# Context tokens' gated projections and mixing laid as filler products between those of norms, expansion, rotation and attention

## The reference, cut to what matters

```python
# first block: h is 272 tokens
h = h + 0.5 * swiglu(rms_norm(h, g_ffn1), ...)
h = h + hybrid_mixer(rms_norm(h, g_mix), ...)   # in_proj, norms, expansion, rope, 16 heads, out
h = h + 0.5 * swiglu(rms_norm(h, g_ffn2), ...)
# second block, layer 0
mod_l = silu_c @ ada_w[0] + ada_b[0]            # shifts, scales and gates of the 256 tokens
mod_c = silu_cc @ ada_w[0] + ada_b[0]           # the same for the 256 context tokens
hl = rmsnorm(x, norm1_g) * (1 + sc1) + sh1
hc = rmsnorm(ctx, norm1_g) * (1 + csc1) + csh1
yl, yc = gmlp_mixer(hl, *gp), gmlp_mixer(hc, *gp)

def gmlp_mixer(h, w_in, b_in, ln_g, ln_b, w_s, b_s, w_out, b_out):
    z = gelu(h @ w_in + b_in)                   # 1024 -> 4096
    u, v = split(z, 2)
    v = layernorm(v, ln_g, ln_b)
    v = einsum('gpq,bcqgd->bcpgd', w_s, v in chunks of 128 tokens, 16 groups) + b_s
    return (u * v) @ w_out + b_out
```

## Time and profile before

| | |
|---|---|
| median of 3 runs | 3289.74 us (3283.09 to 3289.74) |
| profiled execution | 3290.62 us, span 3288.9 us |
| mean granted TensorE clock over the span | 0.912 |
| TensorE busy | 2795.8 us (85% of the span) |
| VectorE, ScalarE, GpSimd busy | 1086.0, 506.4, 320.2 us |

### The profile page before, as it was taken

One profiled execution on the slowest core, in us unless ns is written; L12 is line 12 of the kernel. 1 busy time (PEld: TensorE's weight loads), 2 busy tenths in 40 slices (PEclk: granted clock), 3 DMA queues, 4 the chain that ended last, 5 costly groups with the idle time before them and its releaser, 6 DMA issues. The chain is left out here.

```text
span 3288.9 us, 58163 instructions
## 1 busy us (share of the span) xinstructions
PE 2795.8 (85%) x25453; PEld 1936.1 (59%) x25453; DVE 1086.0 (33%) x2184; ACT 506.4 (15%) x1106; POOL 320.2 (10%) x356
## 2 busy tenths in 40 slices
PE   8998989899998997787777499798888976977775
PEld 7887735788684544444444234388888964544443
DVE  4562363256414412210000321365655522101002
ACT  1000122100110101000000200154444411000001
POOL 1000000000000000211111100042222201111110
PEclk9999755899999998898999799799999987999998
DMA  8684100378523204999999521000000019999994
GB/s 285 225 249 127 39 26 1 128 255 256 153 77 115 64 26 164 347 396 402 404 405 406 182 64 48 18 4 3 4 4 3 4 53 345 403 407 408 405 405 187
DMA packets 279491, 616.54 MB, mean 187 GB/s; under 512 B 28916, under 2 KB 181703, under 8 KB 245204
## 3 DMA queue, kind: packets, MB, share of 16 engines
q1 hardware_dynamic: 237584, 539.56, 44.5%
q10 hardware_dynamic: 30068, 58.82, 5.0%
q0 software_dynamic: 11600, 14.59, 1.4%
HBM read 612.76 MB, written 21.08 MB: 193 GB/s over the span
## 5 line engine op out<-in xcount | busy, mean ns | idle before, releaser
L2076 PE MATMUL bank<-expert_weights,ex_xt 128*64 128x256 f32 x2688 | 314.2, 389 | 92.7 <-DMA expert_weights<-in_moe_w_up_dram 73.4
L2076 PEld LDWEIGHTS bank<-expert_weights,ex_xt 128*64 128x64 f32 x2688 | 215.5, 140 | 206.0 <-issue 136.5
L527 PE MATMUL bank<-u,weights 128*128 128x272 f32 (+1 forms) x1408 | 317.6, 389 | 10.3 <-DVEq L550 10.3
L527 PEld LDWEIGHTS bank<-u,weights 128*128 128x128 f32 x1408 | 269.9, 192 | 57.7 <-DVEq L550 10.9
L1228 DVE SCALAR_TENSOR_TENSOR ada_acc<-ada_w,cond,ada_acc 128x512 f32 (+1 forms) x336 | 227.5, 744 | 1.6 <-PEq L499 1.6
L1987 DVE TENSOR_TENSOR ex_hidden<-ex_silu,bank 128x256 f32<-128x256 f32 x64 | 26.9, 421 | 595.9 <-ACT ex_silu L2125 595.9
L605 PE MATMUL bank<-rw_mixed,weights 128*128 128x512 f32 (+2 forms) x448 | 189.3, 584 | 31.7 <-DVEq L616 28.2
L2076 PE MATMUL bank<-weights,ex_xt 128*64 128x256 f32 x1408 | 166.0, 392 | 35.0 <-DMA weights<-in_moe_w_up_dram 33.6
L2097 PE MATMUL bank<-expert_weights,ex_hidden_turned 128*64 128x512 f32 x672 | 160.3, 621 | 21.7 <-DVE ex_hidden_turned L1990 21.7
L2076 PEld LDWEIGHTS bank<-weights,ex_xt 128*64 128x64 f32 x1408 | 112.2, 141 | 95.3 <-issue 56.5
L605 PEld LDWEIGHTS bank<-rw_mixed,weights 128*128 128x128 f32 (+1 forms) x448 | 84.2, 189 | 137.2 <-issue 135.3
(11 more groups left out here) (550 smaller groups left out, 4138.2 us busy)
## 6 DMA issues: line engine op xcount, KB each, us to landing
expert_weights<-in_moe_w_gate_dram SPq DMA_DIRECT2D x84, 1024.0 KB, 24.5
expert_weights<-in_moe_w_up_dram SPq DMA_DIRECT2D x84, 1024.0 KB, 24.5
expert_weights<-in_moe_w_down_dram SPq DMA_DIRECT2D x84, 1024.0 KB, 24.7
ada_w<-in_ada_w_dram ACTq DMA_DIRECT2D x24, 2048.0 KB, 9.0
weights<-in_moe_w_gate_dram SPq DMA_DIRECT2D x44, 1024.0 KB, 24.2
weights<-in_moe_w_up_dram SPq DMA_DIRECT2D x44, 1024.0 KB, 24.3
weights<-in_moe_w_down_dram SPq DMA_DIRECT2D x44, 1024.0 KB, 24.4
weights<-in_w_gate_dram SPq DMA_DIRECT2D x22, 1024.0 KB, 5.5
```

The source lines that it names most:

```text
L527: last = nc.tensor.matmul(k.bank[b + side * NB][:, 0:N], w[:, f, c * P:(c + 1) * P], rhs[:, f, 0:N], start=(f == 5), stop=(f == 4))
L2076: last = nc.tensor.matmul(half_cols(k.bank[2 + side], t), xt[:, s, f * SLOTS:(f + 1) * SLOTS], w[:, q * 512 + t * 256:q * 512 + t * 256 + ...
```

## The change

The gated block's work for the context tokens, up to the gated product, moves ahead of the first model's attention output.

- The weights' order gets two segments more: cv (8 tiles of w_in's second half) behind in, and cu (8 tiles of the first half) behind expand. w_in is thus read twice, 16 MB more.
- Layer 0's mods are summed by `row_sums` (24 products of 512 columns) in the mix norm instead of by column sums in the four small norms; they are turned and spread at the start of in_proj. `mark` moves from layer 1 to layer 0.
- in_proj also normalizes the context tokens (`csq`, 8 products with ones after its second chunk) into `hc`.
- Class `Ahead` lays the v projection, 128 products of 256 columns (128 columns of stationary), in pieces: 16 in each of fqn, fkn, cq and ckv, 64 in the expansion; and the u projection, 128 products as well: 48 in the row norms, 32 in the rotation, 48 in attention (2, 2, 1, 2, 1 over the units to unit 29). Results are drained by VectorE, from rotation on by ScalarE.
- Gelu of v runs on ScalarE in the expansion, centering and squares in the row norms, the normalizing passes (two of 512 columns a unit) on VectorE in units 0 to 7 of attention. The spatial weights are turned in units 8 to 11 (4 transposes each) and mixed in from unit 13, two products of 128 columns a unit. Gelu of u and the gate lie in attn_out.
- Attention's scores get two PSUM banks instead of three, its mixed values two instead of three; the expansion's values are made between the heads.
- gm_norm, gm_v, gm_u, its norm and the spatial stage handle 256 tokens instead of 512. gm_out reads the two halves from two tensors, as two products of 256 columns.
- One `k.clear()` more stands behind attn_out.

```diff
@@ norm_stage, tensor
             for c in range(kc):
+                if ahead is not None:
+                    ahead.v_pieces(pe, 2)
                 pe.wait_ge(squared, c + 1)
                 last = nc.tensor.matmul(ps, k.ones[:, :], sq[:, c, w], start=(c == 0), stop=(c == kc - 1))
             last.then_inc(summed, 1)
-            if mods is not None and mods.l == 0:
-                mods.sums(mods.share_of_norm)
-            if mods is not None and mods.l == 1:
+            if mods is not None:
                 mods.row_sums(pe)
+            if ahead is not None:
+                ahead.v_pieces(pe, 2 * DC - 2 * kc)
@@ head_norm_stage, tensor
             for c in range(heads):
+                ahead.v_pieces(pe, 2)
                 pe.wait_ge(squared, c + 1)
...
-            if mods is not None:
-                mods.sums(14)
+            ahead.v_pieces(pe, 2 * DC - 2 * heads)
@@ expand_stage, sync and tensor
+            for _ in range(4):
+                ahead.feed_v(sp)
...
             for h in range(HEADS):
+                ahead.v_pieces(pe, DC)
+                if h < 6:
+                    values(h)
@@ row_norm_stage, tensor
                     nc.tensor.matmul(k.bank[n][0:HEADS, 0:N], of[0:r, c, :], sq[0:r, i % 4, 0:N],
                                      start=(c == 0), stop=(c == chunks - 1)).then_inc(summed, 1)
+                    ahead.u_pieces(pe, 1)
+            ahead.u_pieces(pe, 8)
...
+                    nc.tensor.matmul(k.bank[2 + i % 4][0:r, 0:N], to[:, c, 0:r], stat[:, n, 2, 0:N],
                                      start=True, stop=True).then_inc(sent, 1)
+                    ahead.u_pieces(pe, 1 + i % 2)
@@ rope_stage, tensor
                 nc.tensor.matmul(k.bank[n % 4][0:QK, 0:TA], k.rope_turn[0:QK, 0:QK], x[0:QK, h, :],
                                  start=True, stop=True).then_inc(turned, 1)
+                ahead.u_pieces(pe, 2)
@@ attention_stage, tensor
+                if u < 30:
+                    ahead.u_pieces(pe, (2, 2, 1, 2, 1)[u % 5])
+                if 8 <= u < 12:
+                    ahead.turn(pe, u - 8)
+                if 13 <= u < 13 + GC:
+                    ahead.spread(pe, u - 13)
@@ attention_stage, vector
+                if u < 8:
+                    ahead.v_norm(dve, 2 * u, 2 * u + 2)
+                if 14 <= u < 14 + GC:
+                    ahead.keep_spread(dve, u - 14)
@@ class Ahead
+    def feed_v(self, sp):
+        j = self.v_fed
+        self.v_fed += 1
+        sp.wait_ge(self.v_made, 2 * j + 2)
+        self.k.stream.start_number(sp, self.k.seg["cv"].first + j + RING)
...
+    def v_pieces(self, pe, count):
+        k = self.k
+        for _ in range(count):
+            n, f = divmod(self.v_at, DC)
+            j, t = divmod(n, 2)
+            self.v_at += 1
+            if f == 0:
+                if t == 0:
+                    k.stream.wait(pe, k.seg["cv"], j // RING, j % RING)
+                if n >= 8:
+                    pe.wait_ge(self.v_kept, n - 1)
+                elif n >= 4:
+                    pe.wait_ge(self.v_kept, n - 3)
+            last = k.nc.tensor.matmul(self.v_bank(n), self.hc[:, f, t * P:(t + 1) * P],
+                                      k.stream.slot(k.seg["cv"], j)[:, f * 256:(f + 1) * 256],
+                                      start=(f == 0), stop=(f == DC - 1))
+            if f == DC - 1:
+                last.then_inc(self.v_made, 1)
...
+    def spread(self, pe, g):
+        k = self.k
+        if g == 0:
+            pe.wait_ge(self.wt_copied, 4)
+            pe.wait_ge(self.v_normed, 8)
+        else:
+            pe.wait_ge(self.mix_kept, g)
+        for t in range(2):
+            last = k.nc.tensor.matmul(k.bank[6][:, t * P:(t + 1) * P], self.v[:, t, g * P:(g + 1) * P], self.wt[:, g, :],
+                                      start=True, stop=True)
+        last.then_inc(self.mixed, 1)
@@ gmlp_v_stage
-        units = [(j, t) for j in range(seg.tiles) for t in range(4)]
+        units = [(j, t) for j in range(seg.tiles) for t in range(2)]
```

More of the change, by code:

```diff
@@ L407, in place_params, with norm_stage @@
             at += pieces[0][0].shape[0]
-def norm_stage(k, name, src, kc, width, eps, parts, dst, scratch=None, mods=None, loads=None):
+def norm_stage(k, name, src, kc, width, eps, parts, dst, scratch=None, mods=None, loads=None, ahead=None):
     nc = k.nc
@@ L426, in norm_stage @@
             block.sync(loads)
+        if ahead is not None:
+            block.sync(ahead.feed_v)
         @block.scalar
@@ L470, in _ @@
                                                    op0=ALU.mult, op1=ALU.mult).then_inc(ready, 1)
-            if mods is not None and mods.l == 0 and mods.columns == 6 * DC:
-                mods.spread(dve)
+            if ahead is not None:
+                ahead.keep_v(dve)
             if parts[0][3] is not None:
@@ L613, in linear_stage @@
             block.gpsimd(pool)
+        if scalar is not None:
+            block.scalar(scalar)
         def empty(eng):
@@ L776, in _, with row_norm_stage @@
                                                op0=ALU.mult, op1=ALU.mult)
-def row_norm_stage(k, name, sides, per, width, mods=None):
+            ahead.keep_v(dve)
+def row_norm_stage(k, name, sides, per, width, ahead):
     nc = k.nc
@@ L795, in row_norm_stage, with _ @@
         rows = [side[2] for side in sides]
+        @block.sync
+        def _(sp):
+            ahead.feed_u(sp, 0, 3)
         @block.gpsimd
@@ L988, in _ @@
             nc.scalar.activation(g[:, 1, :], g[:, 1, :], ACT.Ln, bias=1.0).then_inc(adone, 1)
+            for _ in range(4):
+                ahead.keep_u_scalar(act)
         @block.vector
@@ L1037, in keys, with _ @@
             return META + (t + 1) * P
+        @block.sync
+        def _(sp):
+            ahead.feed_u(sp, 5, 6)
+            ahead.load_spatial_bias(sp)
+            ahead.feed_u(sp, 6, 8)
         @block.tensor
@@ L1237, in last_share @@
         self.add(dve, self.begun - 1, self.ROUND - self.ROUND // self.rest, self.ROUND)
-    def sums(self, count):
-        nc = self.k.nc
-        for m in range(self.columns, self.columns + count):
-            for v in range(2):
-                last = nc.tensor.matmul(self.k.bank[7][:, 2 * m + v:2 * m + v + 1],
-                                        self.acc[:, v, m * P:(m + 1) * P], self.k.ones[:, 0:1], start=True, stop=True)
-        self.columns += count
-        last.then_inc(self.summed, 1)
-        self.parts += 1
     def mark(self, dve):
@@ L1289, in spread_rows @@
         self.gains()
-    def spread(self, dve):
-        k, nc, l = self.k, self.k.nc, self.l
-        mod = k.mods[l]
-        link = Chain(dve, self.done)
-        dve.wait_ge(self.summed, self.parts)
-        for v in range(2):
-            link(nc.vector.tensor_tensor(mod[:, v, :], k.bank[7][:, v:12 * DC:2],
-                                         param(k, "ada_b", 6 * DC, 6 * DC * l), ALU.add))
-        self.gains()
     def gains(self):
@@ L1322, in ffn @@
+def ffn(k, n, h, u, T, t0, seg, gains, to, acc):
     nc = k.nc
```

458 lines of the change are left out of this document (348 added, 110 removed).

## The result

The changed kernel takes 3250.15 us (median of 4 runs, 3243.80 to 3264.11), the one before 3288.47 us on the same chip (4 runs, 3283.09 to 3289.74). The ratio is 0.9892, 95% interval 0.9863 to 0.9921: 1.1% faster, 38 us where 55 were forecast. The profiled execution took 3252.20 us (span 3250.5) against 3290.62, so the two traces differ by 38.4 us.

A forecast was written before the change was run, and what follows sets the result against it. TensorE was taken as the bound: dense products at full clock in the gated block, narrow ones at half clock earlier. Terms of -121.6 and +66.2 sum to -55.4, so 3290.6 becomes 3235 us; range 3195 to 3268.

The forecast's parts named there:

- rival 4: Weight tiles come late at the doubled pace or in the shared ring, one landing in each of three stages: 3250; chance 0.05.
- the likeliest 3215 to 3250: Whole kernel: the main case, its span from the bound on the gaps and 10 us on attention; chance 0.64.
- a clock of 0.50 in attention: Attention: a sign that would make the forecast wrong, which expected near 1.00 from the expansion to unit 30.
- the row norms with no gap: Row norms: the lower bound, where changes between product shapes cost nothing, +8.7 us instead of +20.1.
- gaps of 0.41 and 0.33: Expansion: a head's gaps at half and full clock, used to claim that attention's gaps keep some 0.77 at full clock.
- rival 3: TensorE stays at 1.2 GHz through attention as well: attention takes 178 us, +67; chance 0.04.
- 2.4 of stall, 0.5 of start: Expansion's start: us lost because the second weight tile is requested only after ckv's last v product; stage +26.7.
- The term of 48.0 us: Row norms: the stage with its filler products and changes of shape, 27.9 us before, so +20.1.
- Rival 1: Gaps between unlike products nearly vanish at full clock in row norms and attention, -11.4 and -19: about 3204; chance 0.16.
- Rival 2: Row norms: the clock falls in parts, spreading with 8-row products takes 44 us instead of 23.5; +24, 3259; chance 0.11.
- forecast at 3.27 us: Attention, units 0 to 7: VectorE sets each unit, 1.7 us plus two normalizing passes of 0.77.
- The faster clock pays for the filler, no more: Attention: full clock offsets the added products, 111 us against 113.5, -2.5.

The follow-up runs named there:

- the first trace: The first profiled execution of the changed kernel, unedited; it took 3252.20 us, against 3290.62 for the kernel before.
- the second: The trace from running the changed kernel again, unedited; that run's median was 3246.73 us, ratio 0.9870 to the kernel before.
- with four edits: Changed kernel plus later w_ukv wait, earlier u bank emptying in attention, one normalizing pass a unit, row norms' filler in blocks: 3222.15 us, 0.9792.
- with six: The four-edit kernel, plus two SyncE transfers issued only in the row norms and two u products ahead of their first sum: 3219.42 us, 0.9795.
- the u bank's edit alone: Changed kernel, with ScalarE in attention emptying each u bank at the end of the unit that finished it: 3238.53 us, 0.9843.

## Why the prediction was right, and where it was off

**The range held, the size was off by 17 us.** The work that leaves was forecast at -121.6 and measured at -124.2: half the units of gm_v and half the columns of gm_u go at the prices of the earlier trace rows, with no tile late at the doubled pace, so rival 4 did not happen there. (gm_out, priced at +0.6, came to -0.5.) The mix norm (+15.3) and in_proj (+1.0), rotation and output projection came within 0.3 us, fqn (15.0), fkn (17.8) and cq (11.6) within 0.4. The measured 3250 lies on the upper edge of the likeliest 3215 to 3250, and that it is not further out is in part luck: that span was given for the gaps between shapes, which were priced right, and 10 us of attention, whereas the time went mostly into stretches at half clock. By one of the prediction's own signs, a clock of 0.50 in attention, it was wrong for a part of that stage. A few of its sums are off by little: 16 x 1.20 is 19.2, not 19.0, the row norms with no gap come to +8.4, not +8.7, gaps of 0.41 and 0.33 are a ratio of 0.80, not 0.77, and 16 pairs of rival 3 come to 174 us, not 178.

**The four norms and the expansion, +4.9.** The step "2.4 of stall, 0.5 of start" was the right mechanism, and the wait measured 3.47. What it lacked was what the wait brings on: the clock fell for 3.4 us behind it. Waiting one head later took 4.0 us away, in the stall and the clock together.

**The row norms, +5.1.** The term of 48.0 us is good for full clock: 47.0 was measured twice, and the two gap prices nearly hold. A round trip beside a sum, put at 0.33, cost 0.30 to 0.33 us, one beside a spreading product, put at 0.40, cost 0.37 (two of them take 1.23 + 1.66 = 2.89 us, of which five times 0.43 are columns), and 24 fewer gave at least 6.3. Rival 1 falls with them. The step that failed is the one that counted the stage at 1.00 throughout. The clock fell at its start for 0, 6.7, 13.6 or 34 us in different traces, for 47.0, 50.1, 53.1 or 62.5 us; 0 and 13.6 were seen with one and the same code. A pair of one narrow sum and one product takes 2.10 us then. Where it fell for 6.7 or 13.6 us the clock came back among these pairs, in the three traces with 34 us only under the u products behind them. Rival 2 had the place of the fall wrong: it is the sums, not the spreading.

**Attention, +8.9.** Two errors of opposite sign. Units 0 to 7 were forecast at 3.27 us by VectorE's work; the MLA half took 47.0 us where the terms add up to 50.3, so VectorE had been priced too high: units 0 to 7 took 21.7 us, 2.7 each. It was the bound all the same (with one pass a unit they took 17.3, the half 39.8). The fox half adds up to 60.8 us in the forecast and took 72.8. Without the waits on the u bank, which the forecast had not seen, it takes 62.2 to 62.4 in five traces and 64.2 in a sixth; with them 72.8 in three, 78.6 and 65.2. The two waits are 1.1 us of the difference to 62.3, the rest is clock. At full clock a fox pair took 7.3 us, as forecast (7.4): the prices of products and gaps were right, the clock was not. "The faster clock pays for the filler, no more" stands: 118.2 us without filler at 0.50, 119.8 with it. Rival 3, the clock down through all of attention, came true for 29 us of the fox half in the first trace and for 42 in the second.

**The opening, +4.2 of the +5.0.** The 48 records of the first norm's sums on TensorE took 5.5 us in the trace of before and 9.4 in that of after. With the same code they took 5.8 in the trace with the later w_ukv wait; of 13 traces with this opening, three are early and ten late. So it varies from one execution to the next; whether the change makes the late case more frequent stays open, as there is one trace of before. The -4.1 us of the later stages also lie in unedited stages, and stay unexplained.

**What stays open.** For two of the falls the runs show what brings them on: the one in the wait for w_ukv (six traces of six with the wait, none of seven without) and the one in the fox half behind the wait of 0.70 us on the u bank (five of five; without the wait none of the six traces with the same spread of u products falls before the last 7 us of the half). Not every such wait does it: one of 0.80 us ahead of the fox half and one of 0.44 in it are not followed by a fall. For the fall at the row norms, idle time is likely but not shown as its cause, and what sets its length is open.
## What to carry to other kernels

Where a stage of narrow products is granted half clock, filler of whole 128*128 products can cost next to nothing. Price it at both clocks, look for what can drop the clock (a stage change, a late tile, a bank not yet emptied), and put filler ahead of these waits. Each change of shape there and back costs 0.3 us, so blocks of filler are worth trying, stage by stage: they saved 6 us in the row norms and lost 25 in attention. The two stages differ in how much of their work is filler (48 u products of 0.43 us are 21 us of the 47 in the row norms, and the same 21 of some 110 in attention); that this is what decides was not tested. When the clock falls by chance, one trace is one draw: two stages differed by 6 us between two traces of one code while others repeated to 0.1. Compare two traces of one code before explaining 5 us.

The experiments' best versions, with four edits and with six, take 3222 and 3219 us, 2.1% under the kernel before, where the change alone gives 1.1 to 1.3%. Their five times spread over 13.8 and 4.9 us; but the five of the kernel with the u bank's edit alone, which has the idle time ahead of the row norms, lie within 4.3 us, so the runs don't show that one is steadier.

## What the runs showed of the hardware

- At full clock, going from a product with 8 columns of stationary to one of 128 and back costs 0.30 to 0.33 us, whether one or four products stand on each side; from 8 rows to 128 and back, 0.37 us.
- Attention with TensorE busy for 115.8 of 122.7 us stayed at 0.50, although 64.7 us ahead of it, up to an idle time of 4.0 us at the stage change, were granted 1.00; with 1.5 u products a unit more, and spreading products or transposes in 20 of the 32 units, it ran at 1.00 for 78.4 us in a row.
- The same code was granted 0.50 for 0 us in one execution and for 13.6 us in another at the same place (row norms), and for 47.6 and 20.4 us in a row from the late fox units on.
- A wait of 3.4 to 3.5 us on TensorE brought 3.4 or 6.8 us at 0.50 in each of six traces, one of 0.70 us in the fox half was followed by a fall in each of five, one of 0.80 us earlier in the same stage in none.
- The opening's 48 records of sums took 5.5, 5.8 or 9.4 us by execution.
